# Latent attention's turned keys moved into a scores' bank, its first queries rotated on VectorE, its last steps re-ordered; neighbourhood scores from split operands

## The reference, cut to what matters

```python
# latent attention, 16 heads of 64 + 32 columns
q = rms_norm(rms_norm(q_lat, q_a_g) @ w_q_b, q_norm_g)           # per head, 96 columns
k = rms_norm(concat(k_nope, k_pe), k_norm_g)
q, k = rotate the last 32 columns of each by cos and sin of the position
sc = q @ k.T * 96 ** -0.5                                         # queries 16:144 and 144:272
o = softmax(causal(sc)) @ v
h = h + o @ w_out

# neighbourhood attention, 8 heads of 64
q, k = rms_norm_2(q), rms_norm_2(k)                               # per head, 64 columns
p = softmax(q @ k.T / 8 + bias, window of 4 rows by 16 columns)
y = p @ v
```

## Time and profile before

| | us |
|---|---|
| median of 3 runs (lowest, highest) | 1131.95 (1130.74, 1133.65) |
| the profiled execution's own time | 1132.25 |
| its span | 1130.6 |
| TensorE matmuls busy | 1100.7 |
| VectorE busy | 761.6 |
| ScalarE busy | 652.5 |
| latent attention's steps | about 471 to 572 of the span |
| third block's input product | about 772 to 899 of the span |

### The profile page before, as it was taken

The page is one execution under the profiler, slowest core; times in us unless marked ns, Lnnn a source line. Parts: engine busy times, 40 slices in busy tenths (PEclk is TensorE's granted clock), DMA queues, the critical chain, the costliest instruction groups (busy, mean ns, idle before and its releaser), DMA issues.

```text
span 1130.6 us, 23885 instructions
## 1 busy us (share of the span) xinstructions
PE 1100.7 (97%) x8919; PEld 1066.4 (94%) x8919; DVE 761.6 (67%) x1131; ACT 652.5 (58%) x1071; POOL 170.9 (15%) x162
## 2 busy tenths in 40 slices
PE   6899999999999999989999999999999999999998
PEld 6899999899999999978799999999989999999998
DVE  7789899768655554558776665555687577666543
ACT  7699989655554444467565554445555656555332
POOL 0434543417000000222020000000002201000000
PEclk9899999999999999989999999999999999999999
DMA  6445454485555555433245555655544556555552
GB/s 231 166 152 170 154 184 150 139 253 168 173 179 170 180 162 179 148 111 114 76 156 198 186 185 174 195 176 181 159 139 143 188 173 190 183 186 188 185 185 93
DMA packets 53226, 189.96 MB, mean 168 GB/s; under 512 B 5920, under 2 KB 7200, under 8 KB 53168
## 3 DMA queue, kind: packets, MB, share of 16 engines
q1 hardware_dynamic: 51408, 182.59, 50.2%
q0 software_dynamic: 1760, 6.59, 1.9%
HBM read 188.07 MB, written 1.08 MB: 167 GB/s over the span
## 4 chain that ended last, share of the span: by engine, by line
PE 80%; DVE 9%; ACT 6%; issue 3%; DMA 1%; POOL 0%; ACTq 0%; SPq 0%; DVEq 0%
PE lin L445 24%; PE lin L447 24%; PE lin L446 24%; DVE w_lo L1333 2%; ACT w_hi L915 1%; DVE cv L1435 1%; PE lin L662 1%; PE lin L663 1%; PE lin L664 1%; ACT dd L1006 1%; DVE sg L1445 1%; DMA acs_bc<-acs_dram 1%; DMA w_raw<-w 0%; ACT pr L1260 0%; ACT cv L992 0%
## 5 line engine op out<-in xcount | busy, mean ns | idle before, releaser
L1333 DVE TENSOR_TENSOR w_lo<-w_raw,w_hi 128x1024 fp32r<-128x1024 f32 (+3 forms) x319 | 385.7, 1211 | 260.8 <-ACT w_hi L915 260.4
L915 ACT ACTIVATE w_hi<-w_raw 128x1024 fp32r<-128x1024 f32 (+2 forms) x343 | 353.2, 1034 | 231.8 <-PE lin L447 227.9
L445 PE MATMUL lin<-x_hi,w_hi 128*128 128x256 f32 (+1 forms) x1504 | 435.2, 289 | 5.9 <-DVE cv L1435 3.2
L447 PE MATMUL lin<-x_hi,w_lo 128*128 128x256 f32 (+1 forms) x1504 | 429.6, 286 | 0.0
L446 PE MATMUL lin<-x_lo,w_hi 128*128 128x256 f32 (+1 forms) x1504 | 429.0, 285 | 0.0
L445 PEld LDWEIGHTS lin<-x_hi,w_hi 128*128 128x128 f32 x1504 | 285.0, 190 | 9.0 <-issue 3.1
L446 PEld LDWEIGHTS lin<-x_lo,w_hi 128*128 128x128 f32 x1504 | 284.5, 189 | 1.4 <-issue 1.0
L447 PEld LDWEIGHTS lin<-x_hi,w_lo 128*128 128x128 f32 x1504 | 285.3, 190 | 0.0
L447 PE MATMUL lin<-hid_hi,w_lo 128*128 128x256 f32 (+1 forms) x768 | 218.2, 284 | 0.0
L446 PE MATMUL lin<-hid_lo,w_hi 128*128 128x256 f32 (+1 forms) x768 | 217.9, 284 | 0.0
L445 PE MATMUL lin<-hid_hi,w_hi 128*128 128x256 f32 (+1 forms) x768 | 217.4, 283 | 0.0
(11 more groups left out here) (280 smaller groups left out, 1489.5 us busy)
## 6 DMA issues: line engine op xcount, KB each, us to landing
w_raw<-w SPq DMA_DIRECT2D x342, 512.0 KB, 3.4
acs_bc<-acs_dram POOLq DMA_DIRECT2D x8, 544.0 KB, 5.2
bias_mask<-rpb POOLq DMA_DIRECT2D x4, 512.0 KB, 9.6
h<-h SPq DMA_DIRECT2D x4, 272.0 KB, 4.1
out<-h SPq DMA_DIRECT2D x8, 128.0 KB, 3.2
cst<-const SPq DMA_DIRECT2D x1, 808.0 KB, 6.7
vecs<-vec SPq DMA_DIRECT2D x1, 131.5 KB, 2.1
w_raw<-w SPq DMA_DIRECT2D x1, 128.0 KB, 5.1
```

The costliest lines, as they stand in the source:

```text
L445: mm3(o, wh, xh, start=first and i == 0, stop=False)
L447: ins = mm3(o, wl, xh, start=False, stop=last and i == kts - 1)
L915: a(w_hi[pg.slot][:, 0:n], w_raw[pg.slot][:, 0:n], ACT.Copy).then_inc(w_hi_done, pages)
L1333: tt(w_lo[pg.slot][:, 0:n], w_raw[pg.slot][:, 0:n], w_hi[pg.slot][:, 0:n].bitcast(F32), ALU.subtract)\
```

## The change

Latent attention:

- `turned_meta` moves from bank 1 of `lin` to the unused columns 416 to 447 of `ps6`, the bank of the odd heads' scores. `key_unit(i)` waits for `kn_done` instead of `kfin_done`; `turn_keys(i)` for i >= 2 waits for the minimum of head 2i-3 (`sm_done`); the odd heads' scores wait for `kfin_done`.
- The rotation of the first three pairs' queries (`FILL_PAIRS = 3`) is made by VectorE, right behind the scaling (`turn_query`: two products of 128 x 128 and two differences of 128 x 64), instead of by GpSimd.
- The sums of `q_stat` go to `ps7` instead of `ps6`, and the first scores no longer wait for their reader.
- On ScalarE, `p_t0_copy` of even steps stands ahead of the rounding of the next page; at t = 16 it stands ahead of `unit_final`; the page rounded in step 15 is rounded in step 16, behind `o_high`.
- On TensorE, the first five-block piece of the output product moves in step 17 from ahead of the transposes and scores to behind them.
- The first page of the output product's third chunk is split in two halves, each with its own rounding, difference and wait.

Third block:

- `qk_stat` becomes two fast-format matmuls on a split square (`sq_hi`, `sq_lo`) against a rounded block matrix. VectorE gets a full product and a difference of 128 x 512 for each of the four chunks; ScalarE squares as before, into `sq_hi`.
- `scores2` becomes twelve fast-format matmuls on `qk_hi` and `qk_lo`. ScalarE gets four roundings and VectorE four differences of 128 x 512, in steps 2 to 5.

```diff
-        turned_meta = lin[0:QK, 1, 256:256 + 2 * META].rearrange("p (h t) -> p h t", h=2)
+        turned_meta = ps6[0:QK, 416:416 + 2 * META].rearrange("p (h t) -> p h t", h=2)
...
             def key_unit(i):
-                    pe.wait_ge(kfin_done, i)
+                    pe.wait_ge(kn_done, i)
...
             def turn_keys(i):
+                if i >= 2:
+                    pe.wait_ge(sm_done, 2 * i - 2)
...
             def scores(n):
+                else:
+                    pe.wait_ge(kfin_done, min(8, (n + 1) // 2 + 1))
...
-                if 17 <= t < 21:
+                if 18 <= t < 21:
                     mout_part(t - 17, 5 if t < 19 else 3, 0)
...
+                if t == 17:
+                    mout_part(0, 5, 0)
...
+            tile(lin[:, 2 * k.parity, 0:T2], c.page(), o_hi, o_lo, T2, kts=4, last=False, half=True)
+            tile(lin[:, 2 * k.parity, 0:T2], c.page(), o_hi, o_lo, T2, kts=4, kt0=4, at=4, first=False)\
+                .then_inc(w_used, 1)
...
             def qk_stat(i):
-                nc.tensor.matmul((ps5, ps6)[i % 2][:, :], blk, qk_sq[i % 2][:, :, :].rearrange("p a t -> p (a t)"),
-                                 start=True, stop=True).then_inc(qkstat_done, 1)
+                nc.tensor.matmul(o, blk_r[:, :], sq_hi[i % 2][:, :], start=True, stop=False)
+                nc.tensor.matmul(o, blk_r[:, :], sq_lo[i % 2][:, :], start=False, stop=True).then_inc(qkstat_done, 1)
...
             def scores2(j):
+                    for i, (q_, k_) in enumerate(((qk_hi, qk_hi), (qk_hi, qk_lo), (qk_lo, qk_hi))):
...
             for t in range(MLA_STEPS + 1):
                 if t >= 8 and t % 2 == 0:
                     o_high((t - 8) // 2)
+                if t == 16:
+                    hi(At(C_HEAD).page(18))
...
+                if t == 16:
+                    p_t0_copy(t - 6)
                 if 1 <= t <= 16:
                     unit_final(t - 1)
-                if t >= 16 and t < MLA_STEPS:
+                if t > 16 and t < MLA_STEPS:
                     p_t0_copy(t - 6)
-                if 1 <= t <= 16:
+                if 6 <= t < 16 and not t % 2:
+                    p_t0_copy(t - 6)
+                if 1 <= t <= 16 and t != 15:
                     nxt = t + 3
...
+            def turn_query(i):
+                dve.wait_ge(qn_done, i + 1)
+                for n in range(2):
+                    tt(q_rot[:, n, :, :], q_n[:, :, HD:QK],
+                       rope_q[:, :, :, 32 * n:32 * n + 32].rearrange("p b h d -> p (b h) d"), ALU.mult)\
+                        .then_inc(qrot_done, 1)
+                dve.wait_ge(qrot_done, 2 * i + 2)
+                for n in range(2):
+                    ins = tt(q_n[:, :, HD + 16 * n:HD + 16 * n + 16], q_rot[:, 0, :, 16 * n:16 * n + 16],
+                             q_rot[:, 1, :, 16 - 16 * n:32 - 16 * n], ALU.subtract)
+                ins.then_inc(qrope_done, 1)
...
+                if i < 4:
+                    tt(qk_sq[i % 2][:, :, :], dst, dst, ALU.mult).then_inc(sqf_done, 1)
+                    tt(sq_lo[i % 2][:, :], qk_sq[i % 2][:, :, :].rearrange("p a t -> p (a t)"),
+                       sq_hi[i % 2][:, :].bitcast(F32), ALU.subtract).then_inc(qksq_done, 1)
+                if 2 <= i < 6:
+                    tt(qk_lo[:, pair, :], qk_f[:, pair, :], qk_hi[:, pair, :].bitcast(F32), ALU.subtract)\
+                        .then_inc(qkl_done, 1)
```

## The result

The changed kernel takes 1122.55 us (median of 4 runs, 1121.39 to 1122.87) against 1131.35 (4 runs) of the kernel before: ratio of the two times 0.9914, 95% interval 0.9898 to 0.9930. Its profiled execution took 1122.35 us with a span of 1120.7, so 9.9 less than the 1130.6 of before, where 7.95 were forecast. The medians are 8.8 apart: the profiled run of before lay 0.9 above its median, and its executions differ in the granted clock (see filled).

What follows compares the result with a forecast made beforehand. TensorE was taken to bound the kernel (80% of the chain), VectorE part of the third block. Savings of 4.9 + 0.65 + 0.6 + 1.65 + 0.15 = 7.95 us from the median 1131.95 gave 1124.0, predicted as 1124.2; range 1121.0 to 1128.0.

Steps and rivals of the forecast that it cites:

- First steps: Latent attention's first steps: of 7.9 us in stalls and clock falls, 4.9 us would be saved (bounds 3.2 and 7.9).
- The full pipeline: Latent attention once its pipeline is full: nothing saved, and the keys' new wait costs nothing while TensorE sets the pace.
- Last steps: Latent attention's end: re-ordered ScalarE and TensorE work shortens waits up to `values(5)`, saving 0.65 us (bounds 0 and 1.5).
- Halved page: Output product's third chunk: a shorter VectorE difference cuts the 0.8 us stall, saving 0.6 us (bounds 0.3 and 0.8).
- `qk_stat`, 1.65: Third block's statistics: fast matmuls save 0.41 us four times, 1.65 us (bounds 1.3 and 1.8), VectorE's added 8.3 us fitting barely.
- The rival built on it: Third block's steps 1 to 5: VectorE's added 8.3 us lie wholly on the path, giving 1134.4 us; chance 0.06.
- `scores2`, 0.15: Third block's scores: each call 0.15 us shorter, only the first counting on TensorE's chain; bounds -1.0 and 0.5.
- more is won: Latent attention: VectorE takes up the full pipeline's slack faster, keeping nearly all of 7.9 us, 1121.3 us; chance 0.10.
- The clock falls again: Latent attention's steps 5 and 17: longer new stalls make TensorE's clock fall, losing 4.4 us, 1128.7 us; chance 0.12.
- VectorE as the bound: Third block's steps 1 to 5: VectorE's extra work sets the pace, 1134.4 us, or 1130.2 for half; chance 0.06.
- the keys' wait in every pair: Full pipeline: `turn_keys` waits 1.5 us for the minimum in six pairs with clock falls, 1143 us; chance 0.02.

Runs made afterwards that it cites:

- filled: The kernel before plus 11 useless matmuls ahead of each of key units 1 to 3, while TensorE waits for `k_fin`; 1129.80 us, ratio 0.9979.
- meta_old: The changed kernel with the turned meta columns back in bank 1 of `lin` and the old waits; 1129.60 us, ratio 0.9982 against the kernel before.
- rot_all: The changed kernel with all eight pairs' queries rotated on VectorE instead of three; 1123.35 us, ratio 0.9925 against the kernel before.
- tail_old: The changed kernel with the last steps' old order on ScalarE and TensorE, including `p_t0_copy`; 1123.41 us, ratio 0.9924 against the kernel before.
- scores2_old: The changed kernel with only `scores2` back to eight slow-format records on unsplit queries and keys; 1123.43 us, ratio 0.9923 against the kernel before.
- third_old: The changed kernel with both `qk_stat` and `scores2` put back as before; 1125.33 us, ratio 0.9943 against the kernel before.
- xlo_whole: The changed kernel with VectorE's last `x_lo` ahead of the next two pages' differences and the third chunk's page whole again; 1122.48 us, ratio 0.9913.
- rot_none: The changed kernel with no pair's queries rotated on VectorE, all eight on GpSimd; 1123.39 us, ratio 0.9924 against the kernel before.

## Why the prediction was right

The direction is as forecast, the size nearly (1124.2 for a measured 1122.55), and all places but one. The sum, 7.95, was 1.8 short of the 9.74 read from the traces: the first steps gave 2.2 more, the third block 0.2 more, the halved page 0.56 less. So the miss on the page is covered by luck, by a larger miss of the other sign. And 0.6 of the 1.65 between forecast and result is the kernel before, whose median is 1131.35 over four runs and was 1131.95 over the three known at the forecast.

- **First steps, 4.9: measured 7.12.** The mechanism was right (meta_old, filled), the clock's part nearly (3.0 of 3.4). The stalls that come in place were mis-sized: of the 7.9 that could be won, 0.8 is lost and not 2.6. The 1.1 in step 5 was 0.2, and TensorE's timeline shows no wait in step 7 where 0.7, 0.3 and 0.2 were forecast. I had put VectorE's instructions end to end with their durations, while they start closer (`k_ss` is 0.55 long, and the next instruction starts 0.47 behind its start, 495.30 and 495.77 in after; the rotation takes 0.81 and not 1.0); by step 7 `q_ss` starts at 499.55, not 501.3. And "TensorE cannot keep a lead over it" was wrong: that period was argued from busy shares, rot_all refutes it.
- **The full pipeline, 0:** right, the period is 9.45 and no keys' wait shows.
- **Last steps, 0.65: measured 0.61** (tail_old 0.62). The `p_t0_copy` in step 7, which the forecast priced at 0.6, is worth 0.38. The new wait of step 17's transposes for `p_t0_copy` is there, 0.6 where about 1.0 was forecast.
- **Halved page, 0.6: measured 0.04.** This step failed. I priced the stall and did not ask who comes next: VectorE's row up to `x_lo` was the later one.
- **`qk_stat`, 1.65: measured 1.60;** VectorE's 8.3 us are covered. With them it is busy 16.5 of 20 us; the forecast's "at most 6.0 of 6.1" a chunk was too high again, and its own terms (4.1 and 3 x 0.7) would have made 6.2, more than the chunk has. The rival built on it should have started from 6.3 won, not 6.15; it did not come.
- **`scores2`, 0.15: the first call gives 0.15,** but E shows 0.38 for all four, so later calls count as well, where I had held that VectorE alone sets the pace (scores2_old also frees VectorE of four differences, so the 0.38 is what is left of both). By the Trainium skill's rule on weight loads (TensorE: Matmul & The Clock Gate, Part 3: they overlap matmuls in flight only for another row group) the call would have been 0.4 longer, an estimate. It is 0.15 shorter, so the rule is not borne out here; the same Part also names a background weight buffer as a way to load early, and no run here shows whether it is at work.
- **The rival "more is won"** had the right mechanism, though it was priced for nearly all of the 7.9. **"The clock falls again"** is real: of 8 profiles with the changed latent attention two (third_old, xlo_whole) show 0.66 in 540 to 545 us and 1.3 us more. It is not in the profile of after. Of all 33 executions of these kernels five have a mean clock of 0.995, the others 0.996 or 0.997, so the chance of 0.12 was not far off; where the clock fell is known for the two profiles alone. **VectorE as the bound** in steps 1 to 5 and **the keys' wait in every pair** did not come.

## What to carry to other kernels

When a stall is removed, follow the engine that ended it until the next thing it owes: the halved page was worth 0.04 us until `x_lo` came earlier, then 0.72. A stretch where one engine is busy 9 of 10 is not yet set by it; moving a product of 0.7 us into its idle wait gained 2 us where taking 3.4 us of work off it gained nothing. Compare stretches between fixed points of two traces rather than spans: where the clock is the same they repeat to about 0.1 us, while spans of the same code moved by 1 to 2.

## What was not expected of the hardware

- Matmuls without use in the stalls made the kernel 2.5 us faster in span and 1.5 by medians, through the granted clock.
- No single length of stall decides on the clock: it held behind a wait of 1.0 us (rot_none), and fell in third_old and xlo_whole behind waits of 0.35 and 0.33 us that after has too, without a fall. What decides between such runs stays open.
- A VectorE instruction on two columns took 0.97 instead of 0.17 us while GpSimd worked on 1024.
